# Two transformer blocks on one core: the second mixer in eight steps of one head pair, each beside the strips of the next pair

## The reference, cut to what matters

```python
proj = h @ w_in                      # 1024 -> 3*512 + 3*512 + 8
# stick-breaking, 8 heads of 64, query blocks of 128
z = q @ k.T * scale
log_keep = where(mask, log_sigmoid(-z), 0)            # mask: key < query
later = cumsum(log_keep, reverse=True) - log_keep
w = where(mask, exp(log_sigmoid(z) + later), 0);  sb_out = w @ v
# forgetting, 8 heads of 64; q and k are RMS-normalised per head
log_f_cum = cumsum(log_sigmoid(fox_f + b_f))
z = fq @ fk.T * scale + log_f_cum[query] - log_f_cum[key]
fox_out = softmax(where(key <= query, z, -inf)) @ fv
x = x + (1 + ga2) * (concat(sb_out, fox_out) @ w_o)
```

## Time and profile before

| | us |
|---|---|
| median of 3 runs | 1961.7 (1960.4 to 1966.1) |
| the profiled execution | 1959.5 |
| its span, first to last instruction | 1957.7 |
| TensorE busy (matmul) | 1901.6, 97% |
| VectorE busy | 991.8, 51% |
| ScalarE busy | 688.4, 35% |
| GpSimd busy | 45.9, 2% |
| mean granted TensorE clock | 0.987 |

### The profile page before, as it was taken

One profiled execution on the slowest core, in us unless ns is written; L12 is line 12 of the kernel. 1 busy time (PEld: TensorE's weight loads), 2 busy tenths in 40 slices (PEclk: granted clock), 3 DMA queues, 4 the chain that ended last, 5 costly groups with the idle time before them and its releaser, 6 DMA issues.

```text
span 1957.7 us, 21498 instructions
## 1 busy us (share of the span) xinstructions
PE 1901.6 (97%) x8929; PEld 1583.3 (81%) x8929; DVE 991.8 (51%) x1335; ACT 688.4 (35%) x1027; POOL 45.9 (2%) x75
## 2 busy tenths in 40 slices
PE   6999999999999999999999999999999999999998
PEld 5688888887888888888888888777778878888887
DVE  5555553457766757753333336246576553333332
ACT  5444442334323323442222224245644442222222
POOL 0000000000000000000000001000021000000001
PEclk9999999999999999889999999999999999999999
DMA  3222222364675665423333332321100123333333
GB/s 120 65 84 86 76 83 86 97 181 135 186 223 176 207 182 179 137 73 98 97 96 98 96 87 78 98 58 40 43 23 1 46 84 97 97 97 97 97 91 92
DMA packets 321718, 200.07 MB, mean 102 GB/s; under 512 B 6696, under 2 KB 311126, under 8 KB 321622
## 3 DMA queue, kind: packets, MB, share of 16 engines
q1 hardware_dynamic: 320128, 196.17, 34.4%
q0 software_dynamic: 640, 2.10, 0.3%
q10 hardware_dynamic: 854, 0.43, 0.1%
HBM read 196.57 MB, written 2.10 MB: 101 GB/s over the span
## 4 chain that ended last, share of the span: by engine, by line
PE 85%; DVE 6%; ACT 4%; DMA 2%; issue 2%; POOL 0%; SPq 0%; DVEq 0%; ACTq 0%
PE ps L1140 84%; DMA w_raw<-in_w_ffn_up 2%; PE ps L1143 1%; ACT w_hi L346 1%; DVE p_lo L1028 1%; DMA w_raw<-in_w_ffn_down 1%; DVE mod_acc L767 0%; DMA x_in<-in_x 0%; DVE t_b L738 0%; DVE att_a L1018 0%; DVE p_hi L1027 0%; ACT att_b L643 0%; DVE t_b L943 0%; ACT y_hi L531 0%; DVE p_lo L863 0%
## 5 line engine op out<-in xcount | busy, mean ns | idle before, releaser
L1140 PE MATMUL ps<-u_hi,w_hi 128*128 128x512 f32 x1688 | 666.5, 395 | 7.7 <-DVE u_lo L726 3.3
L1140 PE MATMUL ps<-u_lo,w_hi 128*128 128x512 f32 x1688 | 660.4, 391 | 0.0
L1140 PE MATMUL ps<-u_hi,w_lo 128*128 128x512 f32 x1688 | 660.3, 391 | 0.0
L705 DVE TENSOR_TENSOR w_lo<-w_raw,w_hi 128x1024 fp32r<-128x1024 f32 (+2 forms) x307 | 365.2, 1190 | 310.0 <-ACT w_hi L346 308.8
L346 ACT ACTIVATE w_hi<-w_raw 128x1024 fp32r<-128x1024 f32 (+2 forms) x307 | 314.4, 1025 | 243.9 <-DMA w_raw<-in_w_down 77.6
L1140 PEld LDWEIGHTS ps<-u_hi,w_hi 128*128 128x128 f32 x1688 | 319.3, 189 | 79.0 <-issue 10.4
L1140 PEld LDWEIGHTS ps<-u_hi,w_lo 128*128 128x128 f32 x1688 | 318.9, 189 | 67.0
L1140 PEld LDWEIGHTS ps<-u_lo,w_hi 128*128 128x128 f32 x1688 | 319.3, 189 | 66.0 <-issue 1.5
L1140 PE MATMUL ps<-y_hi,w_hi 128*128 128x512 f32 x656 | 255.9, 390 | 1.2 <-DVE y_lo L945 1.2
L1140 PE MATMUL ps<-y_hi,w_lo 128*128 128x512 f32 x656 | 255.3, 389 | 0.0
L1140 PE MATMUL ps<-y_lo,w_hi 128*128 128x512 f32 x656 | 255.2, 389 | 0.0
(11 more groups left out here) (257 smaller groups left out, 1484.2 us busy)
## 6 DMA issues: line engine op xcount, KB each, us to landing
mod_raw<-in_w_mod SPq DMA_DIRECT2D x72, 512.0 KB, 4.5
w_raw<-in_w_in SPq DMA_DIRECT2D x71, 512.0 KB, 3.8
w_raw<-in_w_ffn_up SPq DMA_DIRECT2D x44, 512.0 KB, 5.0
w_raw<-in_w_gate SPq DMA_DIRECT2D x44, 512.0 KB, 3.8
w_raw<-in_w_up SPq DMA_DIRECT2D x44, 512.0 KB, 3.8
w_raw<-in_w_down SPq DMA_DIRECT2D x32, 512.0 KB, 3.8
w_raw<-in_w_ffn_down SPq DMA_DIRECT2D x16, 512.0 KB, 5.9
w_raw<-in_w_down SPq DMA_DIRECT2D x16, 384.0 KB, 3.3
```

Source lines behind the costliest of these rows:

```text
L705: e.tensor_tensor(w_lo[u % SLOTS][:, 0:n_k, :], w_raw[u % SLOTS][:, 0:n_k, :], f32(w_hi[u % SLOTS][:, 0:n_k, :]), ALU.subtract).then_inc(l ...
L1140: return e.matmul(out_, lhsT, rhs, start=start, stop=stop, skip_group_check=skip)
```

## The change

The mixer runs in eight steps of one pair (four stick-breaking, four forgetting), and each step runs beside the three strips of the next pair; step 7 runs beside the first three strips of w_o.

- One order of strips, "proj": all of proj_s, then all of proj_f. q, k and v of the next pair are cut straight from PSUM (stage_q, stage_k_both, stage_v) or, for forgetting pairs, through one fq and fk of 128x512. sq, sk, sv and fv are gone.
- Each head of a pair has its own p_hi and p_lo. The two sets of three PSUM banks swap between the steps (slot_banks), and the output of a pair goes to the first bank of its head 0.
- In a stick-breaking step the order on TensorE is: scores 0, scores 1, strip, strip, suffix 0, suffix 1, (in the last of them two head sums,) strip, values 0, values 1, v's transposes.
- In a forgetting step: scores 0, scores 1, strip, strip, transposes 0, transposes 1, two head sums, strip, values 0, values 1, v's transposes. All keep_busy calls of the mixer are gone.
- The gate no longer has products of its own: its rows stand in eight unused rows of k_hi and k_lo (64 to 71 for head 0, 0 to 7 for head 1; k now has a tile for each head), and q_hi has ones in the row of the head; GpSimd writes both.
- w_o's first three strips each run seven of their eight blocks in step 7 (open_strip, in the order HEAD_ORDER) and close after the last pair's output (head_product).
- sb_cut on VectorE takes the copies and differences interleaved, and GpSimd's masks are signalled per bank.

The new orders: first TensorE, then its head sums, then ScalarE and last VectorE in a forgetting step:

```diff
+            for i in range(N_STEPS):
+                u = p0 + 3 * (i + 1)
+                last = i + 1 == N_STEPS
+                if i < N_SB:
+                    for u_qk in (u - 3, u - 2):
+                        e.wait_ge(bank_read[u_qk % 2], u_qk // 2 + 1)
+                else:
+                    e.wait_ge(st_q_lo, 3 * (i - N_SB + 1))
+                    e.wait_ge(aux_set, 4 + 2 * (i - N_SB + 1))
...
+                (sb_scores if i < N_SB else fox_scores)(i, 0)
...
+                elif last:
+                    e.wait_ge(u_lo_set, FILL["heads"] * KC + 5)
+                else:
+                    e.wait_ge(at_out, i)
+                (sb_scores if i < N_SB else fox_scores)(i, 1)
+                if last:
+                    open_strip(0)
+                    fox_turn(i, 0)
+                    open_strip(1)
+                    fox_turn(i, 1)
+                    tri_values(i, 0)
+                    tri_values(i, 1)
+                    open_strip(2)
+                    break
                 unit(u, u_act)
+                if i < N_SB:
+                    unit(u + 1, u_act)
+                    sb_suffix(i, 0)
+                    sb_suffix(i, 1)
+                else:
+                    unit(u + 1, u_act)
+                    fox_turn(i, 0)
+                    fox_turn(i, 1)
+                if i + 1 >= N_SB:
+                    head_totals(i, i + 1 - N_SB)
                 unit(u + 2, u_act)
+                tri_values(i, 0)
+                tri_values(i, 1)
+                project_v(i + 1)
+            e.wait_ge(u_lo_set, (FILL["heads"] + 1) * KC)
+            for c in range(OPEN_STRIPS):
+                head_product(U["w_o"] + c, KC - 1).then_inc(unit_done, 1)
+            for c in range(OPEN_STRIPS, KC):
                 unit(U["w_o"] + c, u_act)
```

```diff
+            def head_totals(i, t):
+                if i < N_SB:
+                    e.wait_ge(sb_exped, 6 * i + 3)
+                else:
+                    e.wait_ge(p_cut, cuts_before(i) + 3)
+                for c in range(2):
+                    e.wait_ge(head_sq, 2 * t + c + 1)
+                    mm(bank(slot_banks(i, 0)[1 + c]), consts[:, C_HEADS:C_HEADS + P], t_b[c][:, :], True, True).then_inc(head_total, 1)
```

```diff
+            for i in range(N_SB, N_STEPS):
+                fox_exp(i, 0)
+                fox_exp(i, 1)
                 cut_hi(u + 2)
+                if not last:
+                    e.wait_ge(st_q_lo, 3 * (i + 1 - N_SB))
+                    take_q(i + 1)
+                fox_cut(i, 0)
...
+                square_q(t)
                 cut_hi(u + 3)
+                square_k(t)
+                fox_cut(i, 1)
+                roots(i, t)
+                cut_hi(u + 4)
+                stage_normed(t)
+                take_v(i + 1)
...
+                e.wait_ge(at_valued, 2 * i + 2)
...
+                stage_v(i + 1)
```

```diff
+            for i in range(N_SB, N_STEPS):
+                fox_peak(i, 0)
+                fox_peak(i, 1)
+                fox_divide(i, 0)
+                fox_divide(i, 1)
+                cut_lo(u + 2)
+                fox_cut(i, 0)
...
+                cut_lo(u + 3)
+                take_k(i + 1)
+                fox_cut(i, 1)
+                cut_lo(u + 4)
+                normalise(t)
+                stage_normed(i + 1)
+                if i + 2 == N_STEPS:
+                    for pos in range(4):
+                        fill_head(pos)
...
+                stage_v(i + 1)
```

More of the change, by code:

```diff
@@ L185, in two_blocks @@
         with ExitStack() as r1:
-            fq, fk, fv, sv = (sb(n, [P, KC // 2, SEQ], F32, r1) for n in ("fq", "fk", "fv", "sv"))
+            heads = sb("heads", [P, 6, SEQ], F32, r1)
+            fq, fk, nf = (sb(n, [P, SEQ], F32, r1) for n in ("fq", "fk", "nf"))
+            f_wide = sb("f_wide", [P, TB, P], F32, r1)
+            gate = sb("gate", [P, 3 * TB * N_FOX], F32, r1)
         with ExitStack() as r1:
@@ L196, in two_blocks @@
         with ExitStack() as r2:
[L197 to L201, removed]
+            p_hi = [sb(f"p_hi{n}", [P, TRI], F32R, r2) for n in range(2)]
+            p_lo = [sb(f"p_lo{n}", [P, TRI], F32R, r2) for n in range(2)]
+        with ExitStack() as r2:
+            out_sb = sb("out_sb", [P, KC, SEQ], F32, r2)
         with ExitStack() as r2:
@@ L544, in scalar, with stage_q, stage_k_both @@
             norm("mix2", U["gate_f"])
+            p0 = U["proj"]
+            NF = TB * N_FOX
+            fa, fe, fl = (gate[:, n * NF:(n + 1) * NF] for n in range(3))
+            def stage_q(q_src, n0):
+                for h in range(2):
+                    rows = slice(HEAD_DIM * h, HEAD_DIM * (h + 1))
+                    e.activation(q_hi[rows, h, :], q_src[rows, :], ACT.Copy, scale=SCALE).then_inc(st_q_hi, 1)
+            def stage_k_both(k_src):
+                e.activation(k_hi[:, 0, :], k_src, ACT.Copy).then_inc(st_q_hi, 1)
@@ new lines, in fox_exp @@
+            def fox_exp(i, n):
+                c0 = 4 + 16 * n
+                nm, den = small[:, c0 + 4:c0 + 8], small[:, c0 + 8:c0 + 12]
+                e.wait_ge(fx_peak, 2 * (i - N_SB) + n + 1)
+                for b in range(TB):
+                    j = TB - 1 - b
+                    ins = e.activation(att[n][:, TRI_OFF[j]:TRI_OFF[j] + TRI_N[j]], tri(slot_banks(i, n), j), ACT.Exp,
+                                       bias=nm[:, b:b + 1], accum_out=den[:, b:b + 1])
+                ins.then_inc(fx_exped, 1)
@@ L636, in fox_exp @@
[L636 to L645, removed]
@@ new lines, in stage_k_both, with stage_k_each @@
+            def stage_k_both(k_src, n0):
+                e.wait_ge(st_q_hi, n0 + 1)
+                return e.tensor_tensor(k_lo[:, 0, :], k_src, f32(k_hi[:, 0, :]), ALU.subtract)
+            def stage_k_each(k_src, n0):
+                for h in range(2):
+                    rows = slice(HEAD_DIM * h, HEAD_DIM * (h + 1))
+                    e.wait_ge(st_q_hi, n0 + h + 1)
+                    e.tensor_tensor(k_lo[rows, h, :], k_src[rows, :], f32(k_hi[rows, h, :]), ALU.subtract).then_inc(st_q_lo, 1)
@@ L1054, in fox_peak, with sb_cut @@
-            def fox_peak(m, pair):
-                n = m % 2
+            def sb_cut(n, ready, n0):
+                first = own[0]
+                for k in range(4):
+                    if k < 3:
+                        _, at, w = PACKED[k]
+                        e.wait_ge(ready, n0 + k + 1)
+                        e.tensor_copy(p_hi[n][:, at:at + w], att[n][:, at:at + w]).then_inc(dve_own, 1)
+                        own[0] += 1
+                    if k:
+                        _, at, w = PACKED[k - 1]
+                        e.wait_ge(dve_own, first + k)
+                        e.tensor_tensor(p_lo[n][:, at:at + w], att[n][:, at:at + w], f32(p_hi[n][:, at:at + w]), ALU.subtract).then_inc(p_cut, 1)
@@ new lines, in vector @@
+            cut_lo(p0 + 4)
+            e.wait_ge(fc_summed, 1)
+            e.wait_ge(pool_set, 9 + 5)
+            for at in (0, HEAD_DIM):
+                e.tensor_copy(f_wide[:, :, at:at + N_FOX], ps[:, 6, 0:NF].rearrange("p (t n) -> p t n", n=N_FOX)).then_inc(fc_set, 1)
+            stage_v(0)
+            for i in range(N_SB):
+                u = p0 + 3 * (i + 1)
+                last = i + 1 == N_SB
+                sb_keep(i, 0)
+                sb_cut(0, sb_masked, 6 * i)
+                sb_keep(i, 1)
+                cut_lo(u + 2)
+                if not last:
+                    stage_q(ubank(u), staged(i)).then_inc(bank_read[u % 2], 1)
+                sb_cut(1, sb_masked, 6 * i + 3)
+                if last:
+                    take_k(i + 1)
+                else:
+                    stage_k_both(ubank(u + 1), staged(i) + 2).then_inc(bank_read[(u + 1) % 2], 1)
+                sb_cut(0, sb_exped, 6 * i)
+                cut_lo(u + 3)
+                sb_cut(1, sb_exped, 6 * i + 3)
+                cut_lo(u + 4)
+                if last:
+                    normalise(0)
+                    stage_normed(i + 1)
+                stage_v(i + 1)
@@ L1325, in tensor, with project_v, sb_scores @@
             mod_columns(3)
+            p0 = U["proj"]
             u = U["gate_f"]
+            NF = TB * N_FOX
+            fl = gate[:, 2 * NF:3 * NF]
+            def project_v(i):
+                e.wait_ge(proj_v, i + 1)
+                for tb in range(TB):
+                    ins = turn(ps[:, (p0 + 3 * i + 2) % 2, tb * P:(tb + 1) * P], v_t[:, tb * P:(tb + 1) * P])
+                ins.then_inc(pv_turned, 1)
+            def sb_scores(i, n):
+                for j in range(TB):
+                    js = slice(j * P, (j + 1) * P)
+                    ins = three(tri(slot_banks(i, n), j), (k_hi[:, 0, js], k_lo[:, 0, js]), (q_hi[:, n, j * P:SEQ], q_lo[:, n, j * P:SEQ]),
+                                j < 3, True, skip=j == 3)
+                ins.then_inc(at_scored, 1)
@@ new lines, in tri_values @@
+            def tri_values(i, n):
+                u_v = p0 + 3 * i + 2
```

(24 more changed lines are left out.)

587 lines of the change are left out of this document (275 added, 312 removed).

## The result

| | before | after |
|---|---|---|
| median, us | 1961.6 (1960.4 to 1966.1, 4 runs) | 1942.7 (1941.7 to 1945.1, 4 runs) |
| profiled execution | 1959.5 | 1942.5 |
| span | 1957.7 | 1940.8 |
| TensorE, VectorE, ScalarE busy | 1901.6, 991.8, 688.4 | 1896.3, 983.9, 681.6 |
| mean granted clock | 0.987 | 0.985 |

The ratio is 0.990, with a 95% interval of 0.988 to 0.992: 19 us faster, clear of the 0.3% of the prediction, and outside its range of 1890 to 1928 us.

What follows compares the result with a forecast made beforehand. TensorE, nearly always busy in the second mixer, was taken as the bound. Savings of 74.8 us less 0.5 + 11.4 + 3.9 + 6.6 gave -52.4, from 1959.5 to 1907 us; range 1890 to 1928, likeliest 1900 to 1915.

Steps and rivals of the forecast that it cites:

- touches only the second mixer: Scope of the forecast: only the stretch from the gate strip to the last output strip was expected to change.
- Stick-breaking steps: Four pair steps, walked through from the first score: 37.9 us each falls to 32.5, no wait left, -21.4 us in all.
- Gate rows: Eight-row copies on GpSimd replacing 64 gate products (-10.2 us); expected to cost nothing unless one takes above 5 us.
- Forgetting stage before: Of its 93.2 us, 84.2 were priced as work and fillers; the other 9.0 were called waiting and counted as saved.
- Wait for the second head sum: Steps 4 to 6: TensorE idles 3.4 us per step for the chain w_hi, w_lo, take of fk, square of fk.
- Staging of q and k: Forgetting steps: the chain of roots, normalising and cuts ends 0.4 us after TensorE would be ready, per step.
- Step 7: Last forgetting step: waits of 0.8 for second scores, 0.5 for transposes, 0.2 for values; +3.9 us with w_o's closing.
- The wait ahead of w_o's fourth strip: Closing of w_o: w_hi and w_lo queued behind two updates of x, 3.7 us against 1.4 of cover, +2.4.
- The clock: Half-clock falls in the mixer: +4 in steps 4 to 6, +1.7 after gate products, +0.9 closing w_o; +6.6, bounds 0 to 17.
- Fillers: 252 filler products of the forgetting stage, 0.12 us each, go: -30.2 us, with 9.0 us of waiting counted separately.
- (c): Rival, chance 0.08: stick-breaking steps keep their 21.4 us because ScalarE or VectorE comes too late for suffix 1; 1928 us.
- (d): Rival, chance 0.03: slower, the clock stays at 1.2 GHz through the forgetting steps, 113 us more; 2013 us.

Runs made afterwards that it cites:

- run 1: The changed kernel with one unused tile of 128 bytes per partition put back ahead of u_hi, nothing else touched; 1905.4 us, ratio to before 0.972.
- run 5: run 1 with fk taken ahead of the cut of p and squared ahead of strip u+3's w_hi, in steps 4 to 6; 1896.8 us, ratio 0.967.
- run 6: run 1 plus 10 filler products ahead of the first head sum and 16 between the two, in steps 4 to 6; 1901.3 us, ratio 0.969.
- run 9: run 5 with w_hi and w_lo of w_o's fourth strip made inside step 7, behind the last cut of p; 1890.7 us, ratio to before 0.964.
- run 7: The kernel before without its 252 filler products in the forgetting stage; 1969.0 us, ratio to before 1.0038.
- 3: The changed kernel with 128 bytes added ahead of the weight slots and 128 more ahead of u_hi; 1907.1 us in one run.
- 4: The changed kernel with a pad of 64 bytes ahead of u_hi; 1947.6 us in one run.
- 8: The changed kernel with a pad of 384 bytes ahead of u_hi; 1908.4 us in one run.
- 11: The changed kernel with a pad of 160 bytes ahead of u_hi; 1948.1 us in one run.
- 12: The changed kernel with its 128 bytes put back between u_lo and y, not ahead of u_hi; 1933.8 us in one run.

## Why the prediction was wrong, and where it was right

- **The step that failed** is the sentence that the change "touches only the second mixer". The diff's list of tiles also lost f_col, 128 bytes ahead of u_hi and next to a tile named align, and the prediction put no price on an address. It cost 37 us (1942.7 - 1905.4), by run 1; of these, 5 lie inside the mixer (324.2 - 319.3) and the rest outside. At 5.7 ns each 7032 strip products would cost 40. Most likely some comes back where weight transfers had been the last to arrive: in the list of lines of the chain, transfers of w_ffn_up have 1.5% (29 us) before and in run 1, and are not listed after. No run tests that.
- **The mixer's sum** was -52.4 us. In run 1, with the address right, the mixer takes 319.3 us against 372.1: -52.8. The kernel takes 1905.4 against the 1907 forecast. In the changed kernel itself it is -47.9, because its strips are slower too. That the sum came out within half a microsecond is in part luck, as its parts erred both ways. By the prediction's own prices the stretch ahead of step 0 should take about 30 us, and run 1 has 27.7; steps 4 to 6 about 104, and run 1 has 105.2 (1362.82 to 1468.06).
- Stick-breaking steps: the walk gave no wait and 31 us. Measured 30.9 each (starts at 1237.07 and 1267.97, and the fourth at 1329.77), no wait. Right. The last of them, with the sums and staging: 33.0 expected, 33.05 measured.
- Gate rows: the eight-row copies on GpSimd, for which no row stood, take 0.6 to 1.4 us each in the changed kernel, and TensorE waits for none of them. Right.
- Forgetting stage before: the 9.0 us called waiting were the rest of a sum. TensorE was idle for 5.7 of the 93.2 us, so in 3.3 of them it was busy, with products priced too low.
- Wait for the second head sum: 3.4 expected, in one piece. Measured are two waits, 1.25 ahead of the first head sum, for the cut of p, which the sum didn't have, and 1.97 ahead of the second, by the chain named; together 3.2 (5.9 + 3.8 in three steps). The size is right, and run 5 shows that chain to be the cause of the second; the first stays there.
- Staging of q and k: 0.4 per step expected; no such wait is seen in steps 4 to 6, only 0.5 ahead of step 4. In run 5, with no fall, it doesn't show either. Too high by 1.2 us in all.
- Step 7: 1.5 us of small waits expected; run 1 shows none, run 5 0.6, run 6 0.8. The wait ahead of w_o's fourth strip: 2.4 expected, 3.1 measured, since the strip also needs the second update of x, which the sum had left out. Together 3.9 expected, 3.1 in run 1, and 3.7 and 3.9 in runs 5 and 6.
- The clock: 4 us for steps 4 to 6 expected, 4.1 by run 6 (5.8 by the profiled executions). For the closing 0.9 was expected, and it cost more: the 120 products there take 30.30 us in run 1 and 27.47 in run 9 without a fall, 2.8 us. The clock as a whole was priced too low: by the stretches of run 1 some 24 us of the mixer run at half clock, close to the 25 that the prediction gave as a sign of being wrong.
- Fillers: counted at -30.2 with the waiting as an extra. Run 7 shows that the two are one thing: without strips in their place, leaving the fillers out costs 7 us.
- The rivals: none named the address. The measured time lies beyond (c), the slowest of the rivals that were still faster, whose condition (steps that stay near 38 us) is not met; (d) needed 118 us at half clock, and the mean over steps 4 to 7 in run 1 is 0.95.

## What to carry to other kernels

Read the list of tiles in a diff as part of the change: a small tile that goes or comes moves everything behind it, and here 128 bytes more or less between weights and activations were worth 1.9% of the whole kernel (32 bytes, in one run, 2.2%). Keep stationary and moving operands a fixed, tested distance apart (here a multiple of 256 bytes), and after any change compare the start-to-start time of a product that was not edited. Here fillers were worth replacing by real work, and not worth removing.

## What the runs showed of the hardware that was not expected

- The start-to-start time of 128x128 by 128x512 fp32r products depends on the distance of the two operand tiles in the partition: 226.8 to 226.9 ns at 286 and 287 times 256 bytes, 232.6 at 128 bytes off and 233.5 at 32 or 64 bytes off (means of the 1428 products), at a granted clock of 1.00 in all. In other stretches 128 bytes off costs as much as 32 or 64 (233.3). It follows the distance, not the start, and each pair by itself (runs 1, 3, 4, 8, 11, 12). What in the hardware does this stays open.
- A single idle of 1.25 us behind 2.3 us of transposes left the clock at 2.4 GHz in all three steps of run 5's profile; together with one of 1.97 a little later, two head sums beside them, the clock was at 1.2 GHz behind it in all three steps of run 1's.
